# Low halves of the weights formed on VectorE, and inverse square roots by a power on GpSimd

## The reference

```python
# first block, 2 layers
h = rms_norm(x, norm_w[layer]);  proj = h @ w_in[layer]          # 1024 x 5376
a = sliding_window_attention(q, k, v, sinks) * silu(z_attn)       # window 128
b = rms_norm(hgrn2_recurrence(q_h, k_h, i_h, logf)) * silu(g_h)   # 4 heads of 128
x = x + (sigmoid(gate_attn) * (a @ w_up_attn) + sigmoid(gate_hgrn) * (b @ w_up_hgrn)) @ w_out
x = rms_norm(x, final_norm_w)
# second block, 2 layers: a mixer (i = 0 top-k index attention, i = 1 differential attention)
# and a squared-relu MLP; mod = silu(c) @ ada_w + ada_b is 2 x 6144
h = x * (1 + sc_t) + sh_t;  x = layer_norm(DN_ALPHA * x + (1 + g_t) * mixer(h))
h = x * (1 + sc_c) + sh_c;  x = layer_norm(DN_ALPHA * x + (1 + g_c) * (square(relu(h @ w1)) @ w2))
```

## Time and profile before

| what | value |
|---|---|
| runs | 1356.48, 1361.79, 1363.51 us; median 1361.79 |
| profiled execution | 1365.75 us, span of its instructions 1364.0 us |
| mean granted TensorE clock | 0.886 of full speed |
| TensorE matmuls | 1132.9 us busy, 83% |
| VectorE, ScalarE | 582.3 and 571.2 us, 43% and 42% |
| GpSimd | 758.3 us, 56%, of which 753.9 in 304 low parts |
| weights and other transfers | 221.59 MB, mean 162 GB/s |

### The profile page before, as it was taken

One profiled execution on the slowest core, in us unless ns is written; L12 is line 12 of the kernel. 1 busy time (PEld: TensorE's weight loads), 2 busy tenths in 40 slices (PEclk: granted clock), 3 DMA queues, 4 the chain that ended last, 5 costly groups with the idle time before them and its releaser, 6 DMA issues.

```text
span 1364.0 us, 15970 instructions
## 1 busy us (share of the span) xinstructions
PE 1132.9 (83%) x6584; PEld 959.6 (70%) x6584; DVE 582.3 (43%) x753; ACT 571.2 (42%) x781; POOL 758.3 (56%) x328
## 2 busy tenths in 40 slices
PE   2789699786796988869889699999699656999994
PEld 0778577665685766658678598888577445999993
DVE  2427633222557242323752455235610554543435
ACT  2455364333545473345442343344324443434342
POOL 1575352744464444646204498889348205699993
PEclk9789799897897998979867799999699668999998
DMA  7365333744462535575302266775287103455540
GB/s 286 109 236 196 123 124 115 243 167 158 176 245 70 186 121 192 158 224 155 124 0 65 98 226 243 273 254 185 84 305 274 63 1 123 128 188 205 177 168 31
DMA packets 101023, 221.59 MB, mean 162 GB/s; under 512 B 11360, under 2 KB 17878, under 8 KB 94806
## 3 DMA queue, kind: packets, MB, share of 16 engines
q1 hardware_dynamic: 95776, 210.29, 45.0%
q10 hardware_dynamic: 5174, 10.28, 2.2%
HBM read 219.48 MB, written 1.07 MB: 162 GB/s over the span
## 4 chain that ended last, share of the span: by engine, by line
PE 67%; DVE 15%; ACT 8%; DMA 4%; issue 3%; POOL 2%; ACTq 1%; SPq 0%; DVEq 0%
PE lin_ps L315 12%; PE lin_ps L316 11%; PE lin_ps L317 11%; PE tmp_ps L322 5%; PE tmp_ps L324 5%; PE tmp_ps L323 5%; PE tmp_ps L370 3%; PE tmp_ps L413 3%; PE lin_ps L322 2%; PE lin_ps L323 2%; PE lin_ps L324 2%; PE lin_ps L451 2%; PE tmp_ps L510 2%; DMA ring<-in_b_w_in 2%; ACT arena L890 2%
## 5 line engine op out<-in xcount | busy, mean ns | idle before, releaser
L789 POOL TENSOR_TENSOR wlo<-ring,whi 128x1024 fp32r<-128x1024 f32 (+2 forms) x304 | 753.9, 2493 | 580.2 <-ACT whi L841 579.2
L841 ACT CAST whi<-ring 128x1024 fp32r<-128x1024 f32 (+2 forms) x304 | 312.6, 1035 | 566.4 <-PE lin_ps L317 269.2
L315 PE MATMUL lin_ps<-whi,hThi 128*128 128x512 f32 (+2 forms) x528 | 214.0, 405 | 26.6 <-POOL wlo L789 12.1
L316 PE MATMUL lin_ps<-wlo,hThi 128*128 128x512 f32 (+2 forms) x528 | 208.3, 394 | 0.0
L317 PE MATMUL lin_ps<-whi,hTlo 128*128 128x512 f32 (+2 forms) x528 | 208.1, 394 | 0.0
L322 PE MATMUL tmp_ps<-hThi,whi 128*128 128x256 f32 x520 | 149.4, 287 | 4.6 <-DVE hTlo L1494 4.6
L323 PE MATMUL tmp_ps<-hTlo,whi 128*128 128x256 f32 x520 | 148.8, 286 | 0.0
L324 PE MATMUL tmp_ps<-hThi,wlo 128*128 128x256 f32 x520 | 148.7, 286 | 0.0
L315 PEld LDWEIGHTS lin_ps<-whi,hThi 128*128 128x128 f32 x528 | 104.7, 198 | 59.2 <-issue 20.7
L322 PE MATMUL lin_ps<-hThi,whi 128*128 128x256 f32 x352 | 107.6, 306 | 30.8 <-POOL wlo L789 18.7
L1559 DVE TENSOR_TENSOR arena<-arena 128x1024 f32<-128x1024 f32 x16 | 42.3, 2646 | 184.1 <-ACT arena L1040 184.1
(11 more groups left out here) (252 smaller groups left out, 1593.1 us busy)
## 6 DMA issues: line engine op xcount, KB each, us to landing
ring<-in_mlp_w SPq DMA_DIRECT2D x64, 1024.0 KB, 5.2
ring<-in_ada_w SPq DMA_DIRECT2D x48, 1024.0 KB, 5.3
ring<-in_w_in SPq DMA_DIRECT2D x40, 1024.0 KB, 5.1
ring<-in_b_w_in SPq DMA_DIRECT2D x12, 1024.0 KB, 5.6
ring<-in_w_out SPq DMA_DIRECT2D x8, 1024.0 KB, 5.0
ring<-in_a_w_in SPq DMA_DIRECT2D x6, 1024.0 KB, 5.3
ring<-in_w_up_hgrn SPq DMA_DIRECT2D x4, 1024.0 KB, 6.2
ring<-in_w_up_attn SPq DMA_DIRECT2D x4, 1024.0 KB, 10.0
```

The lines of the kernel that those rows point to most:

```text
L315: pe.matmul(ps, xh, hi, start=first, stop=False, skip_group_check=True)
L316: pe.matmul(ps, xh, lo, start=False, stop=False, skip_group_check=True)
L789: pool.tensor_tensor(wlo[:, n % PARTS, :, 0:width], ring[:, u % RING, 2 * h:2 * h + 2, 0:width], whi[:, n % PARTS, :, 0:width].bitcast(F32 ...
L841: act.copy(whi[:, n % PARTS, :, 0:width], ring[:, u % RING, 2 * h:2 * h + 2, 0:width]).then_inc(S("high_formed"), 1)
```

## The change

The low parts move from GpSimd to VectorE. VectorE now has an `ahead(name)` of its own, before every wait for a result of TensorE, that forms low parts up to the same point as ScalarE casts high ones. GpSimd forms twelve inverse roots as v to the power -0.5 in one instruction each; ScalarE's Ln and Exp and VectorE's Newton step for them are gone. In the MLP ScalarE still evacuates by relu and then also copies the square to `hbhi`, and VectorE's square reads PSUM times the relu. The rest of the diff replaces `full_tmp_of(dve, ...)` and `full_lin_of(dve, ...)` by `full_tmp(...)` and `full_lin(...)`, which call `ahead` first.

```diff
+            pool.memset(half[:], -0.5).then_inc(S("half"), 1)
...
-            for n, (u, h, width) in enumerate(halves):
-                pool.wait_ge(S("high_formed"), n + 1)
-                pool.tensor_tensor(wlo[:, n % PARTS, :, 0:width], ring[:, u % RING, 2 * h:2 * h + 2, 0:width],
-                                   whi[:, n % PARTS, :, 0:width].bitcast(F32), ALU.subtract
-                                   ).then_inc(S("low_formed"), 1)
+            def rstd(name, v, y):
+
+                pool.wait_ge(S(f"{name}var"), 1)
...
+                pool.tensor_tensor(y, v, power, ALU.pow).then_inc(S(f"{name}rstd"), 1)
+
+            row, one = st[:, 1, :, 0], st[:, 2, :, 0]
+            rstd("f0", row, one)
+            rstd("f0h", st[:, 1], st[:, 2])
...
+            rstd("s3ln", mv[:, :, 1], one)
...
-            def rough_rsqrt(name, v, y, after=None):
-
-                if after:
-                    ahead(after)
-                act.wait_ge(S(f"{name}var"), 1)
-                step(act.activation(y, v, ACT.Ln))
-                act.activation(y, y, ACT.Exp, scale=-0.5).then_inc(S(f"{name}rough"), 1)
...
-                    read(act.activation(flat(hidden[g % 2]), flat(ps), ACT.Relu), f"{name}u{g}")
-                rough_rsqrt(f"{name}ln", mv[:, :, 1], st[:, 2, :, 0], f"{name}y1")
+                    act.activation(flat(hidden[g % 2]), flat(ps), ACT.Relu).then_inc(S(f"{name}relu"), 1)
+                    act.wait_ge(*read_of(f"{name}u{g}"))
+                    if g >= 2:
+
+                        act.wait_ge(*done[f"{name}hb{g - 2}"])
+                    act.copy(flat(hbhi[:, g % 2]), flat(hidden[g % 2])).then_inc(S(f"{name}hbhi"), 1)
+                ahead(f"{name}y1")
...
-            def rsqrt(name, v, y, w):
-
-                dve.wait_ge(S(f"{name}rough"), 1)
-                step(dve.tensor_tensor(w, y, y, ALU.mult))
-                step(dve.tensor_tensor(w, w, v, ALU.mult))
-                step(dve.tensor_scalar(w, w, -0.5, 1.5, ALU.mult, ALU.add))
-                step(dve.tensor_tensor(y, y, w, ALU.mult))
+            formed = [0]
+
+            def ahead(name):
+
+                end, plain = halves_at[name]
+                for n in range(formed[0], min(end + PARTS, len(halves))):
+                    u, h, width = halves[n]
+                    if stuck(u, plain):
+
+                        return
+                    dve.wait_ge(S("high_formed"), n + 1)
+                    dve.tensor_tensor(wlo[:, n % PARTS, :, 0:width], ring[:, u % RING, 2 * h:2 * h + 2, 0:width],
+                                      whi[:, n % PARTS, :, 0:width].bitcast(F32), ALU.subtract
+                                      ).then_inc(S("low_formed"), 1)
+                    formed[0] = n + 1
...
                 variance(f"f{L}", st[:, 0, :, 0], st[:, 1, :, 0], D, EPS)
-                rsqrt(f"f{L}", st[:, 1, :, 0], st[:, 2, :, 0], st[:, 0, :, 0])
+                dve.wait_ge(S(f"f{L}rstd"), 1)
...
+                ahead(f"f{L}qh")
                 dve.wait_ge(*read_of(f"f{L}qh"))
                 dve.nop().then_inc(S("level_ready"), 1)
...
                 differences(1)
+                ahead(f"f{L}kv")
+                ahead(f"f{L}q")
                 for lv in range(1, LEVELS + 1):
...
-                    dve.wait_ge(*read_of(f"{name}u{g}"))
-                    if g >= 2:
-
-                        dve.wait_ge(*done[f"{name}hb{g - 2}"])
+                    ps = flat(full_tmp(f"{name}u{g}"))
                     h = flat(hidden[g % 2])
-                    step(dve.tensor_tensor(h, h, h, ALU.mult))
-                    step(dve.tensor_copy(flat(hbhi[:, g % 2]), h))
+                    dve.wait_ge(S(f"{name}relu"), g + 1)
+                    read(dve.tensor_tensor(h, ps, h, ALU.mult), f"{name}u{g}")
+                    dve.wait_ge(S(f"{name}hbhi"), g + 1)
                     dve.tensor_tensor(flat(hblo[:, g % 2]), h, flat(hbhi[:, g % 2].bitcast(F32)), ALU.subtract
                                       ).then_inc(S(f"{name}act"), 1)
+                    if g:
+                        ahead(f"{name}hb{g - 1}")
...
-            for _ in range(4):
+            for part in ("q0", "k0", "q1", "k1"):
+                ahead(f"s2{part}")
                 ada()
             ada_close()
+            for n in range(2):
+                ahead(f"s2v{n}")
```

More of the change, by code:

```diff
@@ L124, in build_program @@
         lams = sb("lams", [P, 8])
+        half = sb("half", [P, NT, 8])
         csil = sb("csil", [P, KT, ADA_ROWS])
@@ L209, in read_of, with stuck @@
             return S(f"lin_read{half}"), n + 1
+        def stuck(u, plain):
+            return any(event[1] > plain and event[0] is S("w_used")
+                       for event in (v["release"] for v in units[max(0, u - 2 * RING):max(0, u - RING + 1)]))
         def win(w, c0, n, k0=0):
@@ L758, in step @@
                 pool.wait_ge(S("pool_step"), bump("pool_step"))
+            pool.memset(half[:], -0.5).then_inc(S("half"), 1)
+            pool.wait_ge(S("half"), 1)
             step(pool.memset(ident[:], 0.0))
@@ L785, in _ @@
                                ).then_inc(S("levels"), 1)
-            for n, (u, h, width) in enumerate(halves):
-                pool.wait_ge(S("high_formed"), n + 1)
-                pool.tensor_tensor(wlo[:, n % PARTS, :, 0:width], ring[:, u % RING, 2 * h:2 * h + 2, 0:width],
-                                   whi[:, n % PARTS, :, 0:width].bitcast(F32), ALU.subtract
-                                   ).then_inc(S("low_formed"), 1)
+            def rstd(name, v, y):
+                pool.wait_ge(S(f"{name}var"), 1)
+                power = half[:, :, 0] if len(v.shape) == 2 and v.shape[1] == NT else half[:, 0, :] if len(v.shape) == 2 else half[:]
+                pool.tensor_tensor(y, v, power, ALU.pow).then_inc(S(f"{name}rstd"), 1)
+            row, one = st[:, 1, :, 0], st[:, 2, :, 0]
+            rstd("f0", row, one)
+            rstd("f0h", st[:, 1], st[:, 2])
+            rstd("f1", row, one)
+            rstd("f1h", st[:, 1], st[:, 2])
+            rstd("n", row, one)
+            rstd("s0c", row, one)
+            rstd("s0ln", mv[:, :, 1], one)
+            rstd("s1ln", mv[:, :, 1], one)
+            for i in range(NT):
+                rstd(f"s2h{i}", st[:, 1, i, :], st[:, 2, i, :])
+            rstd("s2ln", mv[:, :, 1], one)
+            rstd("s3ln", mv[:, :, 1], one)
         @block.scalar
@@ L1086, in _ @@
                 high_of(f"s0oT{h}", 4 * h)
-            rough_rsqrt("s0ln", mv[:, :, 1], st[:, 2, :, 0], "s0y1")
+            ahead("s0y1")
             mlp("s1", 0)
@@ L1109, in _ @@
                 high_of(f"s2oT{h}", 4 * h, lams[:, 4:5])
-            rough_rsqrt("s2ln", mv[:, :, 1], st[:, 2, :, 0], "s2y1")
+            ahead("s2y1")
             mlp("s3", 1)
@@ L1118, in step, with full_tmp, full_lin @@
                 dve.wait_ge(S("dve_step"), bump("dve_step"))
-            def rsqrt(name, v, y, w):
-                dve.wait_ge(S(f"{name}rough"), 1)
-                step(dve.tensor_tensor(w, y, y, ALU.mult))
-                step(dve.tensor_tensor(w, w, v, ALU.mult))
-                step(dve.tensor_scalar(w, w, -0.5, 1.5, ALU.mult, ALU.add))
-                step(dve.tensor_tensor(y, y, w, ALU.mult))
+            formed = [0]
[3 more added lines that the diff above has]
+                    u, h, width = halves[n]
+                    if stuck(u, plain):
+                        return
[4 more added lines that the diff above has]
+                    formed[0] = n + 1
+            def full_tmp(name):
+                ahead(name)
+                return full_tmp_of(dve, name)
+            def full_lin(name):
+                ahead(name)
+                return full_lin_of(dve, name)
             def variance(name, ss, v, n, eps):
@@ L1475, in _ @@
                     cols = slice(c * HALF, (c + 1) * HALF)
-                    ps = full_lin_of(dve, f"f{L}out{c}")
+                    ps = full_lin(f"f{L}out{c}")
                     read(dve.tensor_tensor(x[:, :, cols], x[:, :, cols], ps, ALU.add), f"f{L}out{c}")
             variance("n", st[:, 0, :, 0], st[:, 1, :, 0], D, EPS)
-            rsqrt("n", st[:, 1, :, 0], st[:, 2, :, 0], st[:, 0, :, 0])
+            dve.wait_ge(S("nrstd"), 1)
             dve.wait_ge(S("lnp_landed"), 32)
@@ L1571, in _ @@
             mixed("s0")
+            ahead("s0misc")
             dve.wait_ge(S("s0css"), 1)
@@ L1575, in _ @@
                               ).then_inc(S("s0cvar"), 1)
-            rsqrt("s0c", st[:, 1, :, 0], st[:, 2, :, 0], st[:, 0, :, 0])
+            dve.wait_ge(S("s0crstd"), 1)
             for i in range(NT):
@@ L1579, in _ @@
             ins.then_inc(S("s0ckvn"), 1)
+            ahead("s0iq")
             for i in range(NT):
@@ L1584, in _ @@
                     W = P * (i + 1)
+                    if i and not g:
+                        ahead("s0q0")
+                    ahead(f"s0idx{i}{g}")
                     dve.wait_ge(*read_of(f"s0idx{i}{g}"))
```

49 lines of the change are left out of this document (21 added, 28 removed).

## The result

The changed kernel takes 1366.6 us (median of nine runs, 1365.8 to 1369.6) beside 1360.3 us for the kernel before in the same nine rounds: a ratio of 1.0048, 95% interval 1.0036 to 1.0060. It is slower by about half a per cent, where 1344 us and a clear gain were forecast; it lies above the top of the range, 1363.

What follows compares the result with a forecast made beforehand. TensorE, busy 83% of the span, was taken as the bound, with idle time and lower clock to gain. Terms -21.0 + 0.1 + 3.0 = -17.9 took 1365.75 to 1347.8, less 3.96 to the median: forecast 1344 us, range 1328 to 1363.

Steps and rivals of the forecast that it cites:

- Level loop: Both layers' level loops: late second half +2.8, rotation's wait -6.3, low halves before the gather +2.5; -1.0 us per layer.
- Rival 3: Level loops: slower by VectorE's order, TensorE's clock falling, deciding at 0.76; about 1394 us at 0.6; chance 0.08.
- Roots: Twelve inverse roots at norms and heads: one GpSimd power, 0.7 us with signal, replaces the ScalarE wait and Newton step; -21.0 us.
- rival 1: Inverse roots: the power is dear, 2.5 us on GpSimd, giving back 17 us; 1361 us, no change; chance 0.08.
- Table loads: ScalarE's roots: a trace row showed no drain behind the 1.28 us load (1344); the skill's 1.38 us drain would give 1332.
- Gate chains: Gate chains of both layers: low halves at the chain's end lengthen waits by 2.75 and 3.9, narrow halves -1.3; +5.35 us.
- LayerNorms and s2's attention: LayerNorm roots -7.6 us, low halves between their residual parts +1.1; roots of s2's heads -4.0, its attention +0.3.
- s2's projections: Four transfer, cast and low-half steps, each 1.3 us faster where three count (-3.9), +0.8 before the modulation; -3.1 us.
- MLPs: Both MLPs: VectorE's and ScalarE's work fits within TensorE's 22.4 us per group; 0 us change.
- The thin cover: Behind an MLP group's first product: 8.3 us of formed halves against 7.3 us until the fourth; 1.0 us spare.
- The clock: New TensorE waits at about six places, level cycles above all, lower its granted clock; half charged, 3.0 us.

Runs made afterwards that it cites:

- mlp_only: The kernel before with only the MLP's edit: square from PSUM on VectorE, its copy to the high part on ScalarE; 1359.9 us, ratio 1.001.
- tuned_gather: The changed kernel with low halves reordered in level loops, gate chains, norms, softmaxes and w_out sums, gathers of the last two levels before the factors; 1297.2 us, ratio 0.955.
- lows_first: The changed kernel with VectorE forming the low halves first in each level-loop cycle, ahead of differences and factors; 1338.1 us, ratio 0.984.

## Why the prediction was wrong

The result is 22.6 us over the forecast. Between the two profiled executions the sum had -17.9 us and the spans differ by +0.9, which is 18.8 of the 22.6; one term, the level loops, is 19.4 off, so the other terms together are right to within a microsecond. The remaining 4 us are the step from the profiled execution of the kernel before to its median, which the changed kernel doesn't have (its profiled execution lies on its median, 1366.63 us). That the rest comes out so closely is partly luck: against the trace of `mlp_only` the rest gains 9.7 us, not 16.5.

- **Level loop: the step that failed.** The sum had -1.0 us per layer: a late second half in two cycles, +2.8, the rotation's wait gone, -6.3, low halves before the gather, +2.5. Measured, layer 0 and 1: the rotation's wait -7.0 each, the waits for low halves +6.9 and +8.0, the wait for the last gather +7.0 each, TensorE's own products -0.3 and +2.8. In all +6.6 and +10.8 us stand in place of -2.0 for both. What was missing is that the four steps in front of the low halves don't run one behind the other: the factors wait for ScalarE's exponential, 2.75 us in the cycle shown and 4.20 in the last. The price was worked out from busy times, with the queue's order but without the waits that stand in that order. The reversed order gave 28 us back. With it the last gather still makes TensorE wait 7.5 us, 4.1 more than in the kernel before; `tuned_gather`, with this gather in front of the factors and their wait, takes 3.3 of that back. Why the exponential comes late in the last cycles stays open: it stands behind a cast that waited 4.6 us for a transfer (4.1 in `lows_first`), and no run takes that wait away.
- **Rival 3** named this place and this order, with a chance of 0.08, but with another mechanism: a clock that falls through the loop. The clock in the loops was 0.92 and 0.89 where it had been 0.90 in both, far from the 0.76 from which the rival decided. It had the place right, and its price counted the clock alone. Waiting did most of it: 6.8 and 8.0 us more per loop, and slower products only in layer 1, 2.8 us.
- **Roots: right within what the runs can tell.** -21.0 forecast. With the low halves back on GpSimd the roots gave -16 (13 to 22 us), and with the roots back on ScalarE the kernel was 19 us slower than the changed one by the medians, 21.0 by the profiled executions. The power took 0.70 us at 2 columns (0.6 taken), but 1.64 at 8 and 2.90 at 16; the last is above both bounds from the trace. So rival 1's price came true for two of the twelve, where VectorE waits 3.0 us each, the heads of the first block, and it waits 1.75 us each at the heads of s2; the other eight waits are 0.8 us. What that cost the kernel wasn't measured apart.
- **Table loads: no drain, though the row was misread.** Behind the load of the earlier trace rows the next activation does not follow at once: it starts at 1108.10, 0.72 us behind the load's end, and waits for VectorE. At s0ln of the kernel before, where nothing else holds it, it does follow at once:

```profile
759.23 1.28 ACT L883 ACT_TABLE_LOAD   x1
760.53 0.21 ACT L883 ACTIVATE st<-st 128x2 f32<-128x2 f32 x1
```

The time from the statistics to the scale fell by 1.8 us there, from 2.59 to 0.81, where 1.9 was taken. The Trainium skill's figure for the drain, about 1.38 us ("ScalarE: Activation LUTs", what ACT_TABLE_LOAD costs), does not fit: 0.02 us lie between load and activation here.

- **Gate chains: the waits right, the total roughly.** The first wait grew from 5.3 to 7.85 us where 8.0 was forecast, the second from 7.9 to 11.4 where 11.8 was. For the stretches +5.35 was forecast and +3.7 measured (0.8 and 2.9); against `mlp_only` it is +6.7. The sum in the forecast is 2.75 + 3.9 - 1.3, the two waits' growth and the narrow halves; the +2.45 that it names before the chain is not in it.
- **LayerNorms and s2's attention: right.** TensorE's waits at the three norms fell by 1.6, 1.3 and 1.6 us and the tail by 1.8, together -6.3 where -6.5 was forecast; -3.6 for the attention where -3.7 stood in the sum.
- **s2's projections: a size off.** -3.1 forecast, -1.1 measured, and nothing against `mlp_only` (54.47 beside 54.43 us). Three of four steps were to be 1.3 us faster; TensorE's longest wait there only fell from 4.1 to 3.6 us.
- **MLPs: right.** The changed kernel's first MLP has TensorE busy 177.1 of 179 us where it was 176.5, and the edit alone changed nothing. The thin cover held.
- **The clock: not seen over the kernel, seen in one loop.** 3.0 us were charged for half of some six new waits. TensorE's busy time fell from 1132.9 to 1127.8 us, with a mean granted clock of 0.895 beside 0.886. In the two loops its products took 2.5 us more, in layer 1 alone; in `lows_first`, with most of the waits gone, they took 7 us less than with the change.

## What to carry to other kernels

Work that moves to an in-order engine must be priced where it stands in that engine's order, with every wait that stands in front of it: a busy share of 55% says nothing of the gathers and norms that queue behind a low half whose cast isn't there. Nor does the idle time in front of low halves: it was 350 us with the change and 366 in `lows_first`, which is 28 us faster. What counts is what stands behind the wait. Put such helper work first in a cycle, when its input is ready, and behind the steps that another engine waits for, not between a step and its wait. And when two parts of a change add up, as here about -16 and +25, measure each: the better one was hidden by the other's order, not by its cost.

## What the hardware showed that was not expected

- A power on GpSimd costs by the column: 0.70 us for 128x2, 1.64 for 128x8 and 2.90 for 128x16, about 0.16 us for each column over some 0.4. A subtraction of 1024 columns took the same engine 2.53.
- Waits of VectorE for its own results are dear in number: 304 low halves, each followed by such a wait and a signal that frees the ring slot, made the kernel 14 us slower (1352.2 beside 1338.1), though the waits were thought to be mostly hidden. The wait itself and the later release aren't told apart.
- The same products of layer 1's loop took TensorE 77.6 us at a granted clock of 0.89 with 19.2 us of waits among them, and 72.7 us at 0.94 with 8.3. The relation is not strict: in layer 0 74.8 us went with 11.1 us of waits and 74.5 with 17.9.
